# An fp32 encoder trunk on one core: the q and k heads are turned by VectorE's block transposes instead of TensorE, and the first two output tiles are interleaved

## Chip, cores and metric

One NeuronCore of one Trainium2 chip. The metric is the device time of one execution in microseconds, the median of several. Lower is better.

## What is computed

Two pre-norm transformer layers over 256 tokens of width 2048, all in float32. The first layer's attention has two kinds of heads: A (8 heads, neighbourhood attention with a bias) and B (8 query heads, 2 key/value heads, with axial rotation). The second layer has C (12 query heads, 4 key/value heads, a window and a sink logit) and D (3 groups of 4 query heads, 4 key/value heads, masked by stride), both with a rotation of the first 32 of 128 dimensions. After each attention comes a SwiGLU block of hidden width 5632.

```
for layer in range(DEPTH):
    xn = rms_norm(x, attn_norm[layer])
    x = x + mixer(xn, w_in, w_out, ...)     # q, k: rms_norm by head, gain, rotation
    x = x + swiglu(rms_norm(x, ffn_norm[layer]), w_gate[layer], w_up[layer], w_down[layer])
```

## The kernel before

**Units and ticks.** All weights (some 390 MB) stream through a ring of four slots. A unit is two chunks of 128 rows by 512 columns of a weight matrix. SP loads it to `w_raw`; ScalarE copies it to `w_hi` in the rounded format that TensorE multiplies fast; VectorE subtracts to get `w_lo` (`split`); TensorE's `unit` then runs 12 matmuls, for 2 token blocks x 2 chunks x 3 products (hi*hi, hi*lo, lo*hi). Eight units make a tile of 512 columns in the input and output projections. ScalarE can split unit u only when TensorE is done with unit u-4, and VectorE follows it, so both run at most some three units ahead of TensorE. One unit is one tick of the attention plan.

**The input projection.** Layer one has 9 tiles (`AB_TILES`: kv_b, q_b, q_b, q_a, k_a, v_a, q_a, k_a, v_a), layer two 10 (`CD_TILES`: k_d, q_d, q_d, q_d, k_c, v_c, q_c, q_c, q_c, v_d). All accumulate in PSUM pair 0. While TensorE multiplies the next tile, a finished q or k tile goes through these steps, `qk_tick(p, n)` being unit n of the tile behind it:
- ScalarE's `evacuate` copies the accumulators to `stage[0]`, scaled by the row's norm. It stands in ScalarE's queue before the split of unit 3, and can start once TensorE is done with the first token block of the tile's last unit. The first matmul of the next tile waits for it (`acc_free`).
- unit 0: ScalarE squares `stage[0]` to `stage[1]`.
- unit 1: VectorE sums the squares by head (L971); GpSimd makes `head_rstd` from them (L1153, L1156).
- unit 2: VectorE scales by `head_rstd` into `stage[2]` (L976) and, but for A's heads, rotates into `stage[0]` (`rotate_axial`, `rotate_partial`).
- unit 3 or 4 (`turn_tick`): TensorE transposes the 4 heads x 2 token blocks by eight matmuls with the identity (L431) into the two banks `t_bank`; one unit later ScalarE copies them to `qt_*` or `kt_*` (L694, L696; A's gains ride on this copy).

VectorE's and ScalarE's `attention(t)` stands in their queues three units behind the split, that is behind `split` of unit t+3.

**Items.** One item is one query head (one slot of three groups for D). `AB_ITEMS` and `CD_ITEMS` give its ticks: scores on TensorE; a tick later VectorE's row maxima; a tick later ScalarE's exponentials; then VectorE's division (`probs`); the transposes of `probs` on TensorE; two ticks later (or one) the product with v; ScalarE's and VectorE's hi/lo split of its result to `ht_hi`, `ht_lo` (L676, L964). Score banks are PSUM 2 to 4, taken in turn.

**The output projection.** Four tiles of 8 units. The first runs beside the last items, and each of its units waits (`ot_ready`) for the heads it reads. Each finished tile goes through `residual_add` (VectorE), four groups of four block transposes one unit apart (`turn`, L882), `residual_hi` and `residual_ssq` (ScalarE), `residual_lo` (VectorE). The same is done behind the down projection. At a change of stage the next stage's units wait for the last tile's `xt_lo` (`tile_split`).

Of the kernel before, what the change touches and what calls it, by code (L numbers as in the profile page):

```python
# [32 lines left out]
P = 128  # L33
# [4 lines left out]
DH = 128  # L38
# [25 lines left out]
AB_ITEMS = ([("b", h, 22 + 2 * h, 27 + 2 * h, 29 + 2 * h) for h in range(8)]  # L64
            + [("a", h, t, t + 4, t + 6) for h, t in enumerate((45, 47, 49, 51, 68, 69, 70, 71))])
CD_ITEMS = ([("d", s, 37 + 4 * s, 42 + 4 * s, 80 + s) for s in range(4)]
            + [("c", h, *ticks) for h, ticks in enumerate(
                [(61, 65, 67), (63, 67, 69), (65, 69, 71), (67, 71, 73), (69, 73, 75), (71, 76, 77), (73, 77, 78),
                 (74, 78, 79), (76, 80, 82), (77, 81, 83), (78, 82, 84), (79, 83, 85)])])
# [6 lines left out]

class Mixer:


    def __init__(self, tiles, items, chunks, fills, heads_before, qk_before, last_users):  # L80
        self.tiles, self.items, self.chunks = tiles, items, chunks
        self.ticks = KU * (len(tiles) + 1)
# [6 lines left out]
        for t in range(self.ticks + 8):  # L89
            for p in self.qk_tiles:  # L90
                if t == self.turn_tick(p):
                    for half in range(2):
                        self.fill["qk", p, half] = fills
                        fills += 1
# [6 lines left out]
        assert not {at for *_, at, _ in items} & {self.turn_tick(p) for p in self.qk_tiles}
# [7 lines left out]
        for n, (kind, h, *_) in enumerate(items):  # L109
            self.banks.append([0, 1, 2] if kind == "d" else [n % 3])  # L110
# [28 lines left out]
def plan():  # L139


    ph, u, a, b, f, th = {}, 0, 0, 0, 2 * XT, 2 * XT
# [3 lines left out]
    for layer, (tiles, items, chunks) in enumerate(((AB_TILES, AB_ITEMS, AB_CHUNKS), (CD_TILES, CD_ITEMS, CD_CHUNKS))):  # L146
        m = Mixer(tiles, items, chunks, f, heads, qk, last_users)
# [5 lines left out]
        u, a, th = u + KU * XT, a + XT, th + 2 * XT  # L153
# [21 lines left out]
def encoder(nc, x, attn_gain, ffn_gain, ab_w_in, ab_w_out, a_gain, a_bias, b_gain, cd_w_in, cd_w_out,  # L175
# [3 lines left out]
    with ExitStack() as ctx:  # L179
# [27 lines left out]
        gain_a = sb("gain_a", [P, 2])  # L207
        sink_sb = sb("sink_sb", [P, 12])
# [1049 lines left out]
```

## Time and profile before

| | |
|---|---|
| median of 3 runs | 2148.21 us (2148.09 to 2148.26) |
| the profiled execution | 2148.37 us, span 2146.6 us |
| TensorE busy | 2129.5 us, 99% |
| VectorE busy | 1380.5 us, 64% |
| ScalarE busy | 1001.7 us, 47% |
| GpSimd busy | 65.8 us, 3% |
| DMA | 399 MB, mean 186 GB/s |

Busy is the union of an engine's instructions. Matmuls overlap in the records (each some 0.39 us long, started 0.23 us apart), so what one costs is read from the distance of starts. "Idle before" is the engine's idle time just before an instruction, with what ended it.

### The profile page before, as it was taken

Reading aid. Unit: us, or ns where it says so; the run is one execution under the profiler, and the core shown is the slowest. Engines: PE = TensorE matmul, PEld = TensorE weight load, DVE = VectorE, ACT = ScalarE, POOL = GpSimd, SP = SyncE. Lnnn points to the kernel's source line nnn. Section 1 sums busy time; section 2 is a strip of 40 time slices with the busy share of each in tenths; the row PEclk is TensorE's granted clock in tenths of the full one; section 3 lists DMA queues with packets and bytes.
Section 4 is the critical chain, followed back from the end, with each engine's and each line's share of the span. In section 5 each row is a group of like instructions: output and inputs, shape, how many; then the busy total and the mean of one; then the engine's idle time right before and its main releaser. Section 6 shows DMA issues by size and latency. Waiting matters only on the chain.

```text
span 2146.6 us, 28247 instructions
## 1 busy us (share of the span) xinstructions
PE 2129.5 (99%) x9540; PEld 1760.2 (82%) x9540; DVE 1380.5 (64%) x1807; ACT 1001.7 (47%) x1270; POOL 65.8 (3%) x55
## 2 busy tenths in 40 slices
PE   8999999999999999999999999999999999999999
PEld 7888888888888888888888778888888888888887
DVE  5755587676666766666666666786676666765443
ACT  6555555444444444444455556454444444444443
POOL 0000010000000000000011010000000000000000
PEclk9999999999999999999999999999999999999999
DMA  8545556666666665555665453466666666656654
GB/s 275 167 147 172 172 176 196 195 183 191 204 195 182 190 204 185 186 190 193 210 192 176 147 158 118 157 199 194 194 183 191 203 195 183 189 189 203 215 201 141
DMA packets 207805, 399.32 MB, mean 186 GB/s; under 512 B 13312, under 2 KB 13568, under 8 KB 207744
## 3 DMA queue, kind: packets, MB, share of 16 engines
q1 hardware_dynamic: 205296, 394.30, 59.4%
q10 hardware_dynamic: 2448, 4.21, 0.6%
q8 instruction: 37, 0.61, 0.1%
q14 instruction: 24, 0.20, 0.0%
HBM read 396.37 MB, written 2.10 MB: 186 GB/s over the span
## 4 chain that ended last, share of the span: by engine, by line
PE 96%; DVE 2%; ACT 1%; issue 0%; POOL 0%; DMA 0%; SPq 0%; ACTq 0%; DVEq 0%
PE psum L411 31%; PE psum L414 31%; PE psum L412 31%; PE psum L501 2%; PE psum L431 1%; PE psum L479 1%; ACT w_hi L578 1%; DVE w_lo L836 1%; DVE turn_sb L882 0%; POOL head_rstd L1156 0%; PE psum L499 0%; DMA x_res<-in_x 0%; ACT xt_hi L621 0%; DVE xt_lo L894 0%; DVE stage L976 0%
## 5 line engine op out<-in xcount | busy, mean ns | idle before, releaser
L836 DVE TENSOR_TENSOR w_lo<-w_raw,w_hi 128x1024 fp32r<-128x1024 f32 x760 | 908.5, 1202 | 625.8 <-ACT w_hi L578 620.4
L578 ACT ACTIVATE w_hi<-w_raw 128x1024 fp32r<-128x1024 f32 x760 | 786.3, 1041 | 937.0 <-PE psum L414 925.1
L411 PE MATMUL psum<-w_hi,xt_hi 128*128 128x512 f32 x2016 | 795.6, 395 | 3.8 <-DVE xt_lo L894 3.6
L414 PE MATMUL psum<-w_hi,xt_lo 128*128 128x512 f32 x2016 | 785.5, 390 | 0.0
L412 PE MATMUL psum<-w_lo,xt_hi 128*128 128x512 f32 x2016 | 784.8, 389 | 0.0
L411 PEld LDWEIGHTS psum<-w_hi,xt_hi 128*128 128x128 f32 x2016 | 378.8, 188 | 83.4 <-DVE xt_lo L894 4.8
L414 PEld LDWEIGHTS psum<-w_hi,xt_lo 128*128 128x128 f32 x2016 | 378.6, 188 | 79.7
L412 PEld LDWEIGHTS psum<-w_lo,xt_hi 128*128 128x128 f32 x2016 | 378.9, 188 | 77.8
L411 PE MATMUL psum<-w_hi,ht_hi 128*128 128x512 f32 x960 | 376.1, 392 | 0.0
L414 PE MATMUL psum<-w_hi,ht_lo 128*128 128x512 f32 x960 | 373.7, 389 | 0.0
L412 PE MATMUL psum<-w_lo,ht_hi 128*128 128x512 f32 x960 | 373.6, 389 | 0.0
L882 DVE STREAM_TRANSPOSE turn_sb<-stage 32x256 f32<-32x256 f32 x544 | 236.9, 436 | 8.8
L411 PEld LDWEIGHTS psum<-w_hi,ht_hi 128*128 128x128 f32 x960 | 180.2, 188 | 37.6
L414 PEld LDWEIGHTS psum<-w_hi,ht_lo 128*128 128x128 f32 x960 | 180.2, 188 | 37.6
L412 PEld LDWEIGHTS psum<-w_lo,ht_hi 128*128 128x128 f32 x960 | 180.2, 188 | 37.4
L909 DVE SCALAR_TENSOR_TENSOR stage<-psum,rstd,stage 128x512 f32<-128x512 f32 x44 | 33.1, 751 | 52.0 <-PE psum L414 52.0
L644 ACT ACTIVATE ht_hi<-turn_sb 128x512 f32 (+1 forms) x44 | 25.4, 625 | 79.1 <-DVE turn_sb L882 79.1
L1163 POOL COPY x_res<-stage 128x1024 f32 x12 | 22.4, 1863 | 922.1 <-DVE stage L867 922.1
L867 DVE TENSOR_TENSOR stage<-psum,x_res 128x512 f32<-128x512 f32 x32 | 22.1, 691 | 30.9 <-PE psum L414 30.9
L621 ACT ACTIVATE xt_hi<-turn_sb,gain_x 128x256 f32 (+1 forms) x48 | 20.5, 499 | 43.4 <-DVE turn_sb L882 43.4
L637 ACT ACTIVATE stage<-psum,rstd 128x512 f32<-128x512 f32 x44 | 30.1, 689 | 18.2 <-PE psum L414 18.2
L1156 POOL TENSOR_TENSOR head_rstd<-head_eps,minus_half 128x8 f32<-128x8 f32 (+1 forms) x15 | 36.3, 2418 | 1.2
(98 smaller groups left out, 606.7 us busy)
## 6 DMA issues: line engine op xcount, KB each, us to landing
w_raw<-in_w_gate SPq DMA_DIRECT2D x176, 512.0 KB, 3.7
w_raw<-in_w_up SPq DMA_DIRECT2D x176, 512.0 KB, 3.8
w_raw<-in_w_down SPq DMA_DIRECT2D x160, 512.0 KB, 4.2
w_raw<-in_cd_w_in SPq DMA_DIRECT2D x80, 512.0 KB, 3.8
w_raw<-in_ab_w_in SPq DMA_DIRECT2D x72, 512.0 KB, 3.7
w_raw<-in_ab_w_out SPq DMA_DIRECT2D x32, 512.0 KB, 3.6
w_raw<-in_cd_w_out SPq DMA_DIRECT2D x32, 512.0 KB, 3.6
w_raw<-in_w_down SPq DMA_DIRECT2D x32, 256.0 KB, 2.6
```

What stands on the lines that cost most here:

```text
L411: nc.tensor.matmul(acc, hi[:, chunk, ts], w_hi[:, slot, c, :], start=first and c == 0, stop=False)
L412: nc.tensor.matmul(acc, hi[:, chunk, ts], w_lo[:, slot, c, :], start=False, stop=False)
L414: mm = nc.tensor.matmul(acc, lo[:, chunk, ts], w_hi[:, slot, c, :], start=False, stop=end)
L501: mm = nc.tensor.matmul(dst, qt[:, qh, tok * P:tok * P + P], kt[:, kh, :], start=kind in "ab", stop=True)
L578: nc.scalar.activation(w_hi[:, slot, 0:n, :], w_raw[:, slot, 0:n, :], ACT.Copy).then_inc(hi_ready, 1)
L637: ins = nc.scalar.activation(stage[0][:, tok, :], ACC[0][:, tok, :], ACT.Silu, scale=rstd[:, 2 * layer + 1, tok:tok + 1])
L644: nc.scalar.activation(ht_hi[:, bass.ds(i * 4 + 2 * half, 2), :], turn_sb[:, 2 * half:2 * half + 2, :], ACT.Copy).then_inc(t_hi, 1)
L836: nc.vector.tensor_tensor(w_lo[:, slot, 0:n, :], w_raw[:, slot, 0:n, :], w_hi[:, slot, 0:n, :].bitcast(F32), ALU.subtract).then_inc(lo_rea ...
L882: ins = nc.vector.transpose(dst[32 * r:32 * r + 32, q], src[32 * q:32 * q + 32, r])
L909: ins = nc.vector.scalar_tensor_tensor(out=stage[1][:, tok, :], in0=ACC[1][:, tok, :], scalar=rstd[:, 2 * layer + 1, tok:tok + 1], in1=sta ...
L1156: nc.gpsimd.tensor_tensor(head_rstd[:, :, 0:nh], head_eps[:, :, 0:nh], half, ALU.pow).then_inc(hrstd_ready, 1)
L1163: nc.gpsimd.tensor_copy(x_res[:, :, bass.ds(n * N, N)], stage[0][:]).then_inc(x_stored, 1)
```

## The change

- `turn_heads`: for each q or k tile VectorE does 16 block transposes of 32 partitions x 8 x 32, four in each of the units 3 to 6 of the next tile, from `stage` straight to `qt_*` and `kt_*`, whose layout is now by token block. TensorE's transposes of q and k heads and ScalarE's copies of them go, and with them the second transpose bank.
- `evacuate` of a q or k tile waits for `qk_turned` of the q or k tile before it.
- A's two gains become one product, which ScalarE multiplies onto `kt_a` in place (`k_scaled`), at unit 7.
- The sum of squares, GpSimd's power and the scaling by `head_rstd` are done by token block, in two halves.
- The four output tiles are written out unit by unit (`OUT_UNITS`): tiles 0 and 1 take turns, four units each, tile 1 in PSUM pair 1; then tiles 2 and 3. Tile 0's four groups of `turn` are done in two units.
- Items start 3 or 4 ticks later; the last 4 (layer one) or 8 (layer two) use two score banks in turn; the second o bank goes; one transpose bank is left for `probs`.
- The last tile's `residual_lo` stands one unit earlier, ahead of `mean_square`.

```diff
-AB_ITEMS = ([("b", h, 22 + 2 * h, 27 + 2 * h, 29 + 2 * h) for h in range(8)]
-            + [("a", h, t, t + 4, t + 6) for h, t in enumerate((45, 47, 49, 51, 68, 69, 70, 71))])
+AB_ITEMS = ([("b", h, 25 + 2 * h, 30 + 2 * h, 32 + 2 * h) for h in range(8)]
+            + [("a", h, t, t + 4, t + 6) for h, t in enumerate((48, 50, 52, 54, 72, 73, 74, 75))])
...
+OUT_UNITS = [(n, k) for half in range(2) for n in range(2) for k in range(4 * half, 4 * half + 4)]
+OUT_UNITS += [(n, k) for n in range(2, XT) for k in range(KU)]
+OUT_END = [max(i for i, (tile, _) in enumerate(OUT_UNITS) if tile == n) for n in range(XT)]
+PAIR_UNITS = 2 * KU
...
-            self.banks.append([0, 1, 2] if kind == "d" else [n % 3])
+            late = n - len(items) + (4 if layer == 0 else 8)
+            self.banks.append([0, 1, 2] if kind == "d" else [n % 3] if late < 0 else [2 + late % 2 * 2])
...
             def attention(layer, t):    # TensorE
                 m = mixers[layer]
-                for q, p in enumerate(m.qk_tiles):
-                    if t == m.turn_tick(p):
-                        _, kind, h0 = m.tiles[p]
-                        pe.wait_ge(qk_normed, m.qk0 + q + 1)
...
-                                transposes(lambda c, tok: src[:, tok, (2 * half + c) * P:(2 * half + c + 1) * P], f)
...
+                    if kind[0] in "qk":    # ScalarE, evacuate
+                        act.wait_ge(qk_turned, m.qk0 + m.qk_rank[p])
...
-                                ins = nc.scalar.activation(qk_dest(kind, h0, half), src, ACT.Copy)
...
+                    if kind == "k_a" and t == m.qk_tick(p, 7):
+                        act.wait_ge(qk_turned, m.qk0 + q + 1)
+                        tile = kt_a[:, h0 // 4].rearrange("p t c i -> p (t c i)")
...
+                        nc.scalar.activation(tile, tile, ACT.Copy, scale=gain_qk[:]).then_inc(k_scaled, 1)
...
+            def turn_heads(layer, q, kind, h0, a):
+                if a == 0:
+                    dve.wait_ge(qk_normed, mixers[layer].qk0 + q + 1)
+                nh = 2 if kind == "kv_b" else 4
+                heads = heads_of(stage[2 if kind in ("q_a", "k_a") else 0], nh)
+                for b in range(4):
+                    src = heads[32 * a:32 * a + 32, :, :, 32 * b:32 * b + 32]
+                    dst = qk_tile(kind, h0)[32 * b:32 * b + 32, :, :, 32 * a:32 * a + 32]
+                    ins = nc.vector.transpose(dst, src)
+                if a == 3:
+                    ins.then_inc(qk_turned, 1)
...
+                    a = t - m.qk_tick(p, 3)
+                    if 0 <= a < 4:
+                        turn_heads(layer, q, kind, h0, a)
...
+                for i in range(len(OUT_UNITS)):    # VectorE
+                    for n in range(XT - 1):
+                        if i == OUT_END[n] + LEAD:
+                            residual_add(layer, "out", n)
+                    split(po["u"] + i, i % RING)
+                    if i < PAIR_UNITS:
+                        attention(layer, KU * len(m.tiles) + i - LEAD)
+                    for n in range(XT - 1):
+                        late = i - OUT_END[n] - LEAD
+                        if n == 0 and 0 <= late < 2:
+                            turn(layer, "out", n, 2 * late)
+                            turn(layer, "out", n, 2 * late + 1)
+                        elif n and 0 <= late < 4:
+                            turn(layer, "out", n, late)
+                        if late == (3 if n == 0 else 5):
+                            residual_lo(layer, "out", n)
...
+                    for tok in range(TOK):    # GpSimd
+                        pool.wait_ge(hssq_ready, TOK * (m.qk0 + q) + tok + 1)
+                        step.then(nc.gpsimd.tensor_scalar(head_eps[:, tok, 0:nh], head_ssq[:, tok, 0:nh], 1.0 / DH, EPS,
+                                                          ALU.mult, ALU.add))
+                        nc.gpsimd.tensor_tensor(head_rstd[:, tok, 0:nh], head_eps[:, tok, 0:nh], minus_half[:, 0:nh],
+                                                ALU.pow).then_inc(hrstd_ready, 1)
```

ScalarE's order at the end of the second layer's second tile (`q_d`, heads 0 to 3); L578 is the split, L666 the evacuation, L683 the squares. Before:

```order
L578 ACTIVATE w_hi<-w_raw 128x1024 [waits unit_used,w_loaded0]
L696 ACTIVATE kt_d<-psum 128x512 [waits t_full] x2
L578 ACTIVATE w_hi<-w_raw 128x1024 [waits unit_used,w_loaded1]
L578 ACTIVATE w_hi<-w_raw 128x1024 [waits unit_used,w_loaded2]
L666 ACTIVATE stage<-psum,rstd 128x512 [waits acc0_done]
L666 ACTIVATE stage<-psum,rstd 128x512 [waits unit_used]
L578 ACTIVATE w_hi<-w_raw 128x1024 [waits unit_used,w_loaded3]
L683 ACTIVATE stage<-stage 128x1024 [waits acc0_free]
```

The same place in the changed kernel (L566, L656 and L673 are the same lines there):

```order
L566 ACTIVATE w_hi<-w_raw 128x1024 [waits unit_used,w_loaded0]
L566 ACTIVATE w_hi<-w_raw 128x1024 [waits unit_used,w_loaded1]
L566 ACTIVATE w_hi<-w_raw 128x1024 [waits unit_used,w_loaded2]
L656 ACTIVATE stage<-psum,rstd 128x512 [waits acc0_done,qk_turned]
L656 ACTIVATE stage<-psum,rstd 128x512 [waits unit_used]
L566 ACTIVATE w_hi<-w_raw 128x1024 [waits unit_used,w_loaded3]
L673 ACTIVATE stage<-stage 128x1024 [waits acc0_free]
```

The copies of the transposed heads are gone, and the evacuation has a second wait.

VectorE's order for a q_d tile, from the scaling on; L836 is the split. Before:

```order
L836 TENSOR_TENSOR w_lo<-w_raw,w_hi 128x1024 [waits hi_ready]
L976 TENSOR_TENSOR stage<-stage,head_rstd 128x1024 [waits hrstd_ready]
L944 TENSOR_TENSOR stage<-stage,partial_sb 128x8x32 [waits dve_step]
L947 TENSOR_TENSOR stage<-stage,partial_sb 128x8x16 x2
L951 TENSOR_TENSOR stage<-stage,cd_gain_sb 128x8x96
L952 TENSOR_TENSOR stage<-stage 128x8x32 [waits dve_step]
L836 TENSOR_TENSOR w_lo<-w_raw,w_hi 128x1024 [waits hi_ready] x7
```

In the changed kernel, where L816 is the split:

```order
L975 TENSOR_TENSOR stage<-stage,head_rstd 128x512 [waits hrstd_ready] x2
L924 TENSOR_TENSOR stage<-stage,partial_sb 128x8x32 [waits dve_step]
L927 TENSOR_TENSOR stage<-stage,partial_sb 128x8x16 x2
L931 TENSOR_TENSOR stage<-stage,cd_gain_sb 128x8x96
L932 TENSOR_TENSOR stage<-stage 128x8x32 [waits dve_step]
L816 TENSOR_TENSOR w_lo<-w_raw,w_hi 128x1024 [waits hi_ready]
L944 STREAM_TRANSPOSE qt_d<-stage 32x8x32 [waits qk_normed]
L944 STREAM_TRANSPOSE qt_d<-stage 32x8x32 x3
L816 TENSOR_TENSOR w_lo<-w_raw,w_hi 128x1024 [waits hi_ready]
L944 STREAM_TRANSPOSE qt_d<-stage 32x8x32 x4
```

Two more such pairs of a split and four transposes follow, then three splits.

VectorE's order in the output stage. Before, every tile's residual has the same form; the last tile's, in the first units of the up projection, layer one:

```order
L867 TENSOR_TENSOR stage<-psum,x_res 128x512 [waits unit_used]
L836 TENSOR_TENSOR w_lo<-w_raw,w_hi 128x1024 [waits hi_ready]
L882 STREAM_TRANSPOSE turn_sb<-stage 32x8x32 [waits acc0_free,t_hi]
L882 STREAM_TRANSPOSE turn_sb<-stage 32x8x32 x3
L836 TENSOR_TENSOR w_lo<-w_raw,w_hi 128x1024 [waits hi_ready]
L882 STREAM_TRANSPOSE turn_sb<-stage 32x8x32 x4
```

The changed kernel from the add of tile 0 to that of tile 1 (L847 is the add, L862 the turn, L874 `residual_lo`):

```order
L847 TENSOR_TENSOR stage<-psum,x_res 128x512 [waits unit_used]
L816 TENSOR_TENSOR w_lo<-w_raw,w_hi 128x1024 [waits hi_ready]
L862 STREAM_TRANSPOSE turn_sb<-stage 32x8x32 [waits acc0_free,t_hi]
L862 STREAM_TRANSPOSE turn_sb<-stage 32x8x32 x7
L816 TENSOR_TENSOR w_lo<-w_raw,w_hi 128x1024 [waits hi_ready]
L862 STREAM_TRANSPOSE turn_sb<-stage 32x8x32 x8
L816 TENSOR_TENSOR w_lo<-w_raw,w_hi 128x1024 [waits hi_ready] x2
L874 SCALAR_TENSOR_TENSOR xt_lo<-turn_sb,gain_x,xt_hi 128x256 [waits t_hi,turned]
L874 SCALAR_TENSOR_TENSOR xt_lo<-turn_sb,gain_x,xt_hi 128x256
L874 SCALAR_TENSOR_TENSOR xt_lo<-turn_sb,gain_x,xt_hi 128x256 [waits t_hi]
L874 SCALAR_TENSOR_TENSOR xt_lo<-turn_sb,gain_x,xt_hi 128x256
L847 TENSOR_TENSOR stage<-psum,x_res 128x512 [waits acc1_done,ssq_done,x_stored]
```

Sixteen transposes lie between three splits, and tile 1's add stands right behind tile 0's `xt_lo`.

## Rows read from the trace of the kernel before

**Rows 1.** The page's first part: busy us (share of the span) x instructions.

```profile
PE 2129.5 (99%) x9540; PEld 1760.2 (82%) x9540; DVE 1380.5 (64%) x1807; ACT 1001.7 (47%) x1270; POOL 65.8 (3%) x55
```

**Rows 2.** Waits view, TensorE: who for whom, us in total, times, longest.

```profile
PE psum L411 <- DVE xt_lo L894: 3.6, 3, 1.2
PE psum L431 <- DVE probs L1027: 1.3, 1, 1.3
PE psum L431 <- DVE stage L938: 0.9, 1, 0.9
...
PE psum L499 <- ACT probs L714: 0.5, 1, 0.5
```

**Rows 3.** Timeline, TensorE: start us, us, instruction; a tile's first two units.

```profile
1105.89 0.39 PE L411 MATMUL psum<-w_hi,xt_hi 128*128 128x512 f32 x1
...
1108.61 0.39 PE L411 MATMUL psum<-w_hi,xt_hi 128*128 128x512 f32 x1
```

**Rows 4.** Timeline, TensorE, around a group of q head transposes.

```profile
1119.27 0.39 PE L414 MATMUL psum<-w_hi,xt_lo 128*128 128x512 f32 x1
1119.50 1.03 PE L431 MATMUL psum<-ident_sb,stage 128*128 128x128 f32 x8
1120.29 0.48 PE L411 MATMUL psum<-w_hi,xt_hi 128*128 128x512 f32 x1
1120.60 0.40 PE L412 MATMUL psum<-w_lo,xt_hi 128*128 128x512 f32 x1
```

**Rows 5.** Groups by line and form, TensorE: busy us, mean ns.

```profile
L431 PE MATMUL psum<-ident_sb,stage 128*128 128x128 f32 x112 | 14.6, 273 | 0.9 <-DVE stage L938 0.9
```

**Rows 6.** Timeline, VectorE, residual's turn at a change of stage.

```profile
342.31 1.77 DVE L882 STREAM_TRANSPOSE turn_sb<-stage 32x256 f32<-32x256 f32 x4
344.10 1.23 DVE L836 TENSOR_TENSOR w_lo<-w_raw,w_hi 128x1024 fp32r<-128x1024 f32 x1
345.35 1.78 DVE L882 STREAM_TRANSPOSE turn_sb<-stage 32x256 f32<-32x256 f32 x4
```

**Rows 7.** Timeline, VectorE, squares, scaling and rotation of a q_d tile.

```profile
1111.11 1.21 DVE L971 TENSOR_REDUCE head_ssq<-stage 128x8 f32<-128x1024 f32 x1
1112.69 1.23 DVE L836 TENSOR_TENSOR w_lo<-w_raw,w_hi 128x1024 fp32r<-128x1024 f32 x1 [0.37 <-ACT w_hi L578]
1115.44 1.23 DVE L976 TENSOR_TENSOR stage<-stage,head_rstd 128x1024 f32<-128x1024 f32 x1 [1.53 <-POOL head_rstd L1156]
...
1118.78 2.35 DVE L836 TENSOR_TENSOR w_lo<-w_raw,w_hi 128x1024 fp32r<-128x1024 f32 x2
```

**Rows 8.** Groups by line and form, GpSimd.

```profile
L1156 POOL TENSOR_TENSOR head_rstd<-head_eps,minus_half 128x8 f32<-128x8 f32 x14 | 35.3, 2518 | 1.2
...
L1156 POOL TENSOR_TENSOR head_rstd<-head_eps,minus_half 128x4 f32<-128x4 f32 x1 | 1.0, 1014 | 0.1
```

**Rows 9.** Timeline, ScalarE, evacuation of a tile.

```profile
1106.09 0.69 ACT L666 ACTIVATE stage<-psum,rstd 128x512 f32<-128x512 f32 x1 [0.67 <-PE psum L414]
```

**Rows 10.** Timeline, VectorE, scaling and axial rotation of q_b.

```profile
67.79 1.23 DVE L976 TENSOR_TENSOR stage<-stage,head_rstd 128x1024 f32<-128x1024 f32 x1 [1.53 <-POOL head_rstd L1156]
...
72.79 2.35 DVE L836 TENSOR_TENSOR w_lo<-w_raw,w_hi 128x1024 fp32r<-128x1024 f32 x2
```

**Rows 11.** Timeline, VectorE, an item of C.

```profile
1271.90 0.15 DVE L1020 TENSOR_TENSOR denom<-denom,sinkexp 128x2 f32<-128x2 f32 x1
...
1272.82 0.68 DVE L1010 TENSOR_REDUCE rowmax<-psum 128x2 f32<-128x512 f32 x1
1273.54 0.23 DVE L1012 TENSOR_SCALAR negmax<-rowmax,neg_sink 128x2 f32<-128x2 f32 x1
```

**Rows 12.** Timeline, TensorE, transposes and product of an item.

```profile
1272.96 0.66 PE L431 MATMUL psum<-ident_sb,probs 128*128 128x128 f32 x4 [1.33 <-DVE probs L1027]
1273.45 1.03 PE L479 MATMUL psum<-cd_pt,v_c 128*128 128x256 f32 x4
1274.32 0.27 PE L499 MATMUL psum<-mask_sb,ident_sb 128*128 128x256 bf16 x1
```

**Rows 13.** Timeline, TensorE, matmuls of the opening.

```profile
12.38 0.63 PE L414 MATMUL psum<-w_hi,xt_lo 128*128 128x512 f32 x1
12.81 0.63 PE L411 MATMUL psum<-w_hi,xt_hi 128*128 128x512 f32 x1
```

More of the change, by code:

```diff
@@ L88, in __init__ @@
         self.fill = {}
[L89 to L94, printed above, removed]
+        for t in range(self.ticks):
             for n, (_, _, _, at, _) in enumerate(items):
@@ L99, in __init__ @@
         self.fills = fills
[L101 removed]
+        self.qk_rank = {p: q for q, p in enumerate(self.qk_tiles)}
         self.pv = sorted(range(len(items)), key=lambda n: (items[n][4], n))
@@ L146, in plan @@
     for layer, (tiles, items, chunks) in enumerate(((AB_TILES, AB_ITEMS, AB_CHUNKS), (CD_TILES, CD_ITEMS, CD_CHUNKS))):
-        m = Mixer(tiles, items, chunks, f, heads, qk, last_users)
+        m = Mixer(layer, tiles, items, chunks, f, heads, qk, last_users)
         mixers.append(m)
@@ L376, in _ @@
             for layer in range(2):
-                for p, (col, _, _) in enumerate(mixers[layer].tiles):
+                m = mixers[layer]
+                for p, (col, _, _) in enumerate(m.tiles):
                     for k in range(KU):
@@ L749, in _ @@
                 m, pi, po, pu, pd = mixers[layer], *(ph[s, layer] for s in ("in", "out", "up", "down"))
-                def out_tile(n, first):
-                    for k in range(KU):
-                        if k == LEAD and first:
-                            evacuate(layer, len(m.tiles) - 1)
-                        split(n * KU + (po["u"] + k), k % RING)
-                        if first:
-                            attention(layer, KU * len(m.tiles) + k - LEAD)
-                        elif k == LEAD + 2:
-                            residual_ssq(layer, "out", n - 1)
-                        elif k == LEAD + 3:
-                            residual_hi(layer, "out", n - 1)
                 for p in range(len(m.tiles)):
@@ L1037, in _ @@
                 m, pi, po, pu, pd = mixers[layer], *(ph[s, layer] for s in ("in", "out", "up", "down"))
-                def out_tile(n, first):
-                    for k in range(KU):
-                        if k == LEAD - 1 and not first:
-                            residual_add(layer, "out", n - 1)
-                        split(n * KU + (po["u"] + k), k % RING)
-                        if first:
-                            attention(layer, KU * len(m.tiles) + k - LEAD)
-                        elif LEAD - 1 <= k < LEAD + 3:
-                            turn(layer, "out", n - 1, k - LEAD + 1)
-                        elif k == LEAD + 4:
-                            residual_lo(layer, "out", n - 1)
                 for p in range(len(m.tiles)):
```

234 lines of the change are left out of this document (108 added, 126 removed).

## Prediction

> **What bounds the kernel now.** I read the page's first part, then who TensorE waits for, then the timelines of TensorE, VectorE, ScalarE and GpSimd around one tile. The page says that TensorE is busy 2129.5 of 2146.6 us [rows 1]. The waits view says that behind the opening it waits a handful of times only: 3.6 us in three waits on `xt_lo`, 1.3 on `probs`, 0.9 on a q tile that VectorE had not rotated in time, 0.5 on an exponential [rows 2]. So whatever leaves TensorE's queue shortens the program by its full length, and whatever makes TensorE wait lengthens it by its full length. VectorE is at 64% over the span [rows 1], but that mean says nothing here: the question is whether it is in time at the few points where TensorE waits for it. The unit of all sums is the tick: one weight unit of 12 matmuls, 1105.89 to 1108.61, so 2.72 us [rows 3].
>
> **What is taken off TensorE.** A tile's eight q/k head transposes sit between matmuls. Two matmuls of the stream start 0.23 us apart; around a group the starts are 1119.27, 1119.50 (the group), 1120.29, 1120.60 [rows 4]: 1.33 us from the last before to the second after, where 0.46 would do, so 0.87 a group. The 112 transposes [rows 5] are 14 groups, 12.2 us, and k/v of B with four transposes gives about 0.45 more: **12.7 us**. The waits of 0.9 (it is the wait of such a group), 1.3 and 0.5 go with their places: up to **2.7 us**. ScalarE loses 30 copies out of PSUM and gains two scalings; TensorE does not wait for these copies, so I cost that at nothing; what covers them is ScalarE's idle time.
>
> **The three late `xt_lo`.** The last tile's `residual_lo` now stands one unit earlier, ahead of `mean_square`, at the three changes of stage where TensorE waits 3.6 us in all [rows 2]. VectorE had a free unit there, so I take the **3.6 us** as gone (bounds 0 and 3.6).
>
> **What is put on VectorE.** 16 block transposes a tile, four in each of the units 3 to 6. The nearest rows are the same instruction with the same 32x256 shape in the residual's turn: a group of four takes 1.80 us from its start to the next split (342.31 to 344.10), the split itself 1.25 (344.10 to 345.35) [rows 6]. So a unit with a turn in it takes VectorE 3.05 us, and the tick is 2.72: **during the four units VectorE can't make up lateness, it loses another 0.33 a unit**. The Trainium skill, VectorE: DVE Perf Modes, "The three transpose paths" and "Rules for kernel authors", says that VectorE transposes 32x32 blocks only and advises TensorE for 128x128 where PSUM will do. Its rule speaks against the change in direction; the rows put the same exchange at 0.87 us of TensorE against 7.2 us of VectorE [rows 4, 6].
>
> **The new wait.** ScalarE's `evacuate` of a q or k tile now waits for `qk_turned` of the tile before, since the block transposes read `stage` directly where eight TensorE transposes had freed it at unit 4. The next tile's first matmul waits for that evacuation (one accumulator pair). The deadline is thus TensorE's end of the tile. Worked on the second tile of the second layer (q_d, heads 0 to 3), behind which TensorE starts the third at 1105.89 [rows 3]:
> - VectorE's sum of squares starts at 1111.11; the scaling by `head_rstd` starts at 1115.44, behind GpSimd's power; the rotation ends at 1118.78 [rows 7]. The halves by token help: the power takes 2.52 us for 8 values and 1.01 for 4 [rows 8]. With 0.68 for half the squares, 0.38 for the step before the power and 1.2 a power, the second token's value is there at 1114.8 (1111.11 + 0.68 + 0.38 + 1.2 + 0.2 + 1.2). Its scaling (0.65) and the rotation's 2.1 follow: the end is about 1.1 earlier than now, at 1117.65.
> - Four units with turns: 4 x 3.05 = 12.2, so `qk_turned` comes at 1129.85.
> - Evacuation of the first token 0.69 [rows 9] and two hand-overs of about 0.05 to 0.1: 1130.7.
> - TensorE, without its group of transposes, would be ready for the fourth tile at 1105.89 + 8 x 2.72 = 1127.65.
>
> **It waits 3.05 us to save 0.87.** Bounds: 4.2 where the halved power brings nothing, 2.3 where no power is waited for (squares, split, scaling, rotation back to back). Four tiles of the second layer are like this (k_d and the three q_d): **12.2 us**.
>
> The other tiles, by the same sum plus VectorE's items and minus TensorE's:
> - q_b heads 0 to 3: the axial rotation is longer (67.79 to 72.79, 5.00 against 3.34 for the partial one, so 1.66 more) [rows 7, 10]: **4.7**.
> - q_b heads 4 to 7: 4.7, plus 2.6 us of VectorE item work, less about 4 us of TensorE item work between the units: **3.4**.
> - q_a and the first k_a: rotation none, many items on TensorE: 0. kv_b is half a tile: 0.
> - second k_a: the tile behind it is v, without the wait, but ScalarE scales `kt_a` first (about 1.05) and then evacuates: 1.0 for the wait, 1.05 for the scaling: **2.0**.
> - c tiles (three q_c): VectorE's item work is 0.92 us for reciprocal and two scalings and about 0.9 for the maxima [rows 11], with a split and a turn 4.9 a unit; TensorE has 2.72 plus 0.87 for each product with v and 0.5 for a transpose [rows 12]. Where an item comes every tick this is 4.1. Both sides are close; d3's probabilities now fall beside a q tile's squares; score banks are reused after two items instead of three. I work out about 2.2 for d3's `probs`, 3.4 at the first q_c and 6 from there to the end of the heads: **11.5**, the weakest term (3 to 18).
> - Output tiles: tile 0's four turn groups are done in two units, tile 1 ends four units behind tile 0 and not eight. From tile 0's last matmul VectorE needs 0.75 + 1.2 + 3.6 + 1.2 + 3.6 + 1.2 = 11.6 us until unit 16 is split, which TensorE wants after 4 x 2.72 = 10.9; then `residual_lo`, the wait for ScalarE's sum of squares and tile 1's turns at 3.05 a unit with no reserve left. I get 3.5 a layer, **7.0** (3 to 12).
>
> **Sum.** Waits 12.2 + 4.7 + 3.4 + 2.0 + 11.5 + 7.0 = 40.8; savings 12.7 + 2.7 + 3.6 = 19.0. Net **+21.8 us** on the profiled execution's 2148.37, which is 0.16 over the median of 2148.21: **2170 us**. The small ends (9.2, 3.9, 2.6, 1.2, 3, 3: 23 us of waits) give 2152, the large ones (16.8, 5.9, 4.5, 2.9, 18, 12: 60 us) 2189. A measurement of this kernel tells about 0.2% (4.3 us) from no change.
>
> **Rivals.**
> 1. *The turns are in time* (faster). Mechanism: `qk_turned` comes before TensorE's end of the tile, so only the savings remain: 2148.2 - 19.0 = 2129; with the two output tiles' waits 2136. It decides at a group of four transposes of 1.05 us: 1117.65 + 4 x (1.25 + 1.05) + 0.8 = 1127.65. The shape's 1.8 [rows 6] speaks against it, and nothing in the profile for it but that source and destination differ a little from the residual's. Chance 0.09.
> 2. *The gaps also cost the clock.* TensorE would idle 3 to 5 us some eight times; the longest idle time of before outside the opening is far shorter. At the opening, behind idle time, matmuls start 0.43 us apart (12.38, 12.81) [rows 13], the lower level of 1.2 GHz, against 0.23. If each long gap brings some eight matmuls at that pace, 0.2 us more for each, 8 x 1.6 = 13 us: 2183. The Trainium skill, TensorE: Matmul & The Clock Gate, "Why this matters for your kernels", warns that idle gaps between bursts of matmuls bring the lower clock back. By that rule this rival holds wherever a gap is long enough; no row of this trace has such a gap between matmuls, so it is open. Chance 0.15.
> 3. *Savings and waits cancel.* The waits come out at the small end or below since the items' work on TensorE covers them in both layers: 2144 to 2152. Against it stands that the four d tiles have no item beside them at all. Chance 0.07.
> 4. That the change doesn't do what it says is ruled out by the order: no transpose of `stage` is left on TensorE.
>
> **Numbers.** The forecast, with its own range 2152 to 2188, has 0.69. Range 2148 to 2189. Faster by over 0.2% 0.09 (rival 1), within 0.2% 0.05, slower 0.86.
>
> **What would show it.** In the changed kernel: waits of TensorE on ScalarE's evacuation at the start of the q_d tiles and k_c, some 3 us each, and ScalarE waiting on VectorE's transposes just before; the transposes at 0.44 us, 240 of them; the power of 4 values near 1.2 us; no wait on `xt_lo`; PEclk at 1.0 throughout, or not (rival 2); waits on `w_lo` behind unit 16 of the output stage. I am wrong if the four d tiles start on time, or if the block transposes take about half of what the residual's take.

## The result, and the profile after

| | before | after |
|---|---|---|
| median | 2148.24 us (2148.09 to 2149.57, 4 runs) | 2187.89 us (2187.61 to 2189.43, 4 runs) |
| ratio | | 1.0185, 95% interval 1.0167 to 1.0202 |
| the profiled execution | 2148.37 us, span 2146.6 | 2187.92 us, span 2185.7 |

The change costs 39.6 us. The forecast was 2170; the time lies 18 us above it, at the upper end of the range. The page's first part, as [rows 1]:

```profile
PE 2133.8 (98%) x9424; PEld 1754.6 (80%) x9424; DVE 1484.4 (68%) x2077; ACT 988.4 (45%) x1243; POOL 81.5 (4%) x85
```

TensorE has 116 instructions fewer and is yet 4 us longer busy: something in it got slower. VectorE has 104 us more. Who TensorE waits for, as [rows 2] (us in total, times, longest):

```profile
PE psum L425 <- ACT stage L656: 27.4, 8, 5.8
...
PE psum L445 <- DVE probs L1027: 4.0, 3, 1.8
PE psum L425 <- DVE w_lo L816: 3.2, 5, 0.9
PE psum L425 <- DVE stage L847: 3.0, 2, 1.5
PE psum L425 <- ACT v_a L654: 2.2, 1, 2.2
```

The evacuation (L656), for which the waits view of before has no row, is now waited for eight times, 27.4 us. The wait on `xt_lo` L894 has no successor. Now the second layer's first tile, `k_d`, whose heads VectorE turns while TensorE multiplies the next tile (q_d, heads 0 to 3). VectorE's timeline (start us, us, instruction, idle before):

```profile
1102.52 1.27 DVE L968 TENSOR_REDUCE head_ssq<-stage 128x4 f32<-128x512 f32 x2
...
1106.82 0.69 DVE L975 TENSOR_TENSOR stage<-stage,head_rstd 128x512 f32<-128x512 f32 x1 [0.90 <-POOL head_rstd L1152]
...
1109.62 1.22 DVE L816 TENSOR_TENSOR w_lo<-w_raw,w_hi 128x1024 fp32r<-128x1024 f32 x1
1110.76 1.78 DVE L944 STREAM_TRANSPOSE kt_d<-stage 32x256 f32<-32x256 f32 x4
1112.55 1.23 DVE L816 TENSOR_TENSOR w_lo<-w_raw,w_hi 128x1024 fp32r<-128x1024 f32 x1
1113.81 1.78 DVE L944 STREAM_TRANSPOSE kt_d<-stage 32x256 f32<-32x256 f32 x4
...
1118.66 1.23 DVE L816 TENSOR_TENSOR w_lo<-w_raw,w_hi 128x1024 fp32r<-128x1024 f32 x1
1119.91 1.79 DVE L944 STREAM_TRANSPOSE kt_d<-stage 32x256 f32<-32x256 f32 x4
```

No idle time stands between 1106.82 and 1121.70 (a third split and group are left out): the groups come 3.05 us apart, as worked out from [rows 6]. ScalarE's timeline at the same place:

```profile
1121.74 1.26 ACT L656 ACTIVATE stage<-psum,rstd 128x512 f32<-128x512 f32 x2 [4.08 <-DVE kt_d L944]
```

And TensorE's timeline, from the last matmul of q_d, heads 0 to 3, on:

```profile
1118.84 0.39 PE L428 MATMUL psum<-w_hi,xt_lo 128*128 128x512 f32 x1
1122.57 0.77 PE L425 MATMUL psum<-w_hi,xt_hi 128*128 128x512 f32 x1 [3.35 <-ACT stage L656]
1123.14 0.63 PE L426 MATMUL psum<-w_lo,xt_hi 128*128 128x512 f32 x1
1123.56 0.63 PE L428 MATMUL psum<-w_hi,xt_lo 128*128 128x512 f32 x1
1123.99 0.63 PE L425 MATMUL psum<-w_hi,xt_hi 128*128 128x512 f32 x1
...
1125.64 0.40 PE L426 MATMUL psum<-w_lo,xt_hi 128*128 128x512 f32 x1
1125.87 0.39 PE L428 MATMUL psum<-w_hi,xt_lo 128*128 128x512 f32 x1
```

TensorE is done with that tile at 1119.2, ScalarE is held until the last transpose, and the next matmul starts 3.73 us after the last one. Then comes the second cost: the matmuls behind the gap start 0.43 us apart (1123.14, 1123.56, 1123.99), as in [rows 13], and only from 1125.64 on 0.23 apart. The windows view shows it as a granted clock (stretch, its length, busy us of PE, PEld, DVE, ACT and POOL, then PEclk, DMA share, GB/s):

```profile
1118.84:1122.57 3.73, 0.39 (x2) 0.03 (x1) 3.63 (x6) 0.83 (x2) 0.00 (x0) 0.94 0.64 204
1122.57:1125.50 2.93, 2.93 (x7) 2.35 (x8) 1.62 (x2) 2.33 (x3) 0.00 (x0) 0.50 0.58 157
1125.50:1145.59 20.09, 20.09 (x89) 16.62 (x89) 15.96 (x27) 7.42 (x7) 3.25 (x4) 1.00 0.52 150
```

0.50 is 1.2 GHz, 1.00 is 2.4. Behind the opening there are seven such stretches, each behind an idle gap: of 5.01 us (q_b, heads 0 to 3), 5.79 (q_b, heads 4 to 7), 2.19 (`v_a`) and 3.34 or 3.35 (the four D tiles). 48 matmuls of the stream start some 0.43 us apart in them. A gap of 3.05 us at the first q_c and one of 1.85 before it are followed by none.

### The profile page after: what moved, and what is told of

It is laid out like the page before. It is cut to its first block, busy times and chain, and to the rows that moved or that the text cites. A ratio compares the mean times of both kernels' runs of the same rounds, so it can differ in the third digit from the quotient of the medians.

```text
span 2185.7 us, 27698 instructions
## 1 busy us (share of the span) xinstructions
PE 2133.8 (98%) x9424; PEld 1754.6 (80%) x9424; DVE 1484.4 (68%) x2077; ACT 988.4 (45%) x1243; POOL 81.5 (4%) x85
## 4 chain that ended last, share of the span: by engine, by line
PE 85%; DVE 11%; ACT 2%; POOL 1%; issue 1%; DMA 0%; SPq 0%; ACTq 0%; DVEq 0%
PE psum L425 27%; PE psum L428 27%; PE psum L426 27%; DVE w_lo L816 3%; DVE turn_sb L862 1%; PE psum L471 1%; PE psum L494 1%; POOL head_rstd L1152 1%; DVE qt_d L944 1%; DVE qt_c L944 1%; ACT w_hi L566 1%; PE psum L445 1%; DVE qt_b L944 1%; POOL head_eps L1150 0%; DVE stage L975 0%
## 5 line engine op out<-in xcount | busy, mean ns | idle before, releaser
L816 DVE TENSOR_TENSOR w_lo<-w_raw,w_hi 128x1024 fp32r<-128x1024 f32 x760 | 909.6, 1202 | 573.8 <-ACT w_hi L566 567.6
L566 ACT ACTIVATE w_hi<-w_raw 128x1024 fp32r<-128x1024 f32 x760 | 786.3, 1040 | 953.4 <-PE psum L428 928.5
L425 PE MATMUL psum<-w_hi,xt_hi 128*128 128x512 f32 x2016 | 797.6, 396 | 27.8 <-ACT stage L656 27.4
L862 DVE STREAM_TRANSPOSE turn_sb<-stage 32x256 f32<-32x256 f32 x544 | 236.9, 436 | 8.7
L847 DVE TENSOR_TENSOR stage<-psum,x_res 128x512 f32<-128x512 f32 x32 | 21.7, 690 | 33.6 <-PE psum L428 33.6
L609 ACT ACTIVATE xt_hi<-turn_sb,gain_x 128x256 fp32r<-128x256 f32 (+1 forms) x48 | 20.5, 498 | 52.4 <-DVE turn_sb L862 52.4
L1152 POOL TENSOR_TENSOR head_rstd<-head_eps,minus_half 128x4 f32<-128x4 f32 (+1 forms) x30 | 33.7, 1123 | 2.5
L1164 POOL COPY x_res<-stage 128x1024 f32 x4 | 7.4, 1859 | 693.5 <-DVE stage L847 693.5
```

Of the source, the lines that this page charges most:

```text
L425: nc.tensor.matmul(acc, hi[:, chunk, ts], w_hi[:, slot, c, :], start=first and c == 0, stop=False)
L566: nc.scalar.activation(w_hi[:, slot, 0:n, :], w_raw[:, slot, 0:n, :], ACT.Copy).then_inc(hi_ready, 1)
L816: nc.vector.tensor_tensor(w_lo[:, slot, 0:n, :], w_raw[:, slot, 0:n, :], w_hi[:, slot, 0:n, :].bitcast(F32), ALU.subtract).then_inc(lo_rea ...
L862: ins = nc.vector.transpose(dst[32 * r:32 * r + 32, q], src[32 * q:32 * q + 32, r])
L1152: nc.gpsimd.tensor_tensor(head_rstd[:, tok, 0:nh], head_eps[:, tok, 0:nh], minus_half[:, 0:nh], ALU.pow).then_inc(hrstd_ready, 1)
```

## The experiments

Each time is a median beside runs of the kernel before on the same chip (2148.73 in the first set, 2148.76 in the others). The changed kernel's 2187.89 stood beside 2148.24, so a difference to it, as given below, is uncertain by that 0.5 us.

**1. Keep TensorE at work in the gaps.** Ahead of the waiting first matmul stand matmuls whose result nobody reads, into a PSUM bank that is free.

```diff
+                        if k == 0:
+                            fill_in(FILL.get((layer, p), 0))
                         unit(pi["u"] + t, k % RING, xt_hi, ...)
```

> The changed kernel with 8 to 22 extra matmuls (each 0.23 us, into a bank that nothing reads) in TensorE's queue ahead of the eight first matmuls that wait for an evacuation, and one of v_a: work in place of idle time, deadlines unchanged. Theory (idle gaps cost twice, once as waiting and once because the clock falls behind them): the granted clock is 1.00 throughout, the idle time left at these places is about 1 us or less each, the time falls by the price of 27.3 us at half the clock, some 13 us, to about 2175. Rival (the low clock of the changed kernel lies in idle time and costs nothing): no gain, 2188 or a little more for fillers that come late.

Measured: 2187.93 us (2186.92 to 2188.25), no gain. The forecast failed because two of the eight groups stood at tiles that wait for nothing, where they cost 4.4 and 2.6 us of work, and two real gaps (5.81 and 3.04 us) stayed open, each with a stretch at the lower level of 6.8 us behind it. The time is the one that the rival named, but not for its reason, so it settled nothing; it was repeated with the groups at the right tiles.

```diff
-            FILL = {(0, 2): 20, (0, 3): 22, (0, 9): 8, (1, 2): 13, (1, 3): 13, (1, 4): 13, (1, 5): 13, (1, 7): 12}
+            FILL = {(0, 3): 22, (0, 4): 24, (0, 9): 8, (1, 2): 14, (1, 3): 14, (1, 4): 14, (1, 5): 14, (1, 8): 13}
```

> The changed kernel with fillers (matmuls whose result nobody reads) ahead of the first matmul of the tiles that wait, this time at the right ones: 22 at q_b 0's evacuation, 24 at q_b 4's, 8 at v_a's, 14 at each of the four D tiles, 13 at the first q_c, and none where nothing waits. In the first version two of eight groups stood at tiles that do not wait. They cost 4.4 and 2.6 us, and two of the uncovered gaps kept 13.6 us of the lower clock level, against 27.3 us in all in the changed kernel, so gain and cost cancelled. My theory (13.6 us of the changed kernel's time is the clock behind the long gaps, the rest is waits): no interval of the lower level before the end, waits as before but filled, 2174 (2172 to 2178). Rival (fillers only shift where the clock drops, or the waits are longer than they look): 2183 or more with the lower level still present.

Measured: 2178.02 us (2176.95 to 2180.24), 9.9 less than the changed kernel and at the upper edge of the forecast (2172 to 2178), ratio to before 1.0136 (1.0120 to 1.0151). The windows view at `k_d`'s end, first of the changed kernel, then with fillers:

```profile
1118.00:1130.00 12.00, 8.65 (x33) 6.77 (x32) 7.93 (x12) 4.46 (x6) 0.00 (x0) 0.86 0.59 174
```

```profile
1118.00:1130.00 12.00, 11.83 (x53) 9.48 (x52) 8.16 (x11) 6.34 (x7) 3.25 (x4) 1.00 0.68 186
```

All seven stretches at the lower level are gone. Set side by side unit by unit, the two traces differ in the first unit behind each gap: 1.45, 1.79, 1.59, 1.37, 1.59, 1.58 and 1.60 us, **11.0 us** in all. The distance from the last matmul of the stream before a gap to the first behind it is the same in both (3.73 and 3.73 us at `k_d`), so the fillers change nothing but the pace behind it. One new stretch came, against the forecast, behind a gap of 1.85 us ahead of late probabilities, and costs 1.6. The 11.0 us are the clock's share. My 13.6 was half of the 27.3 us in which the lower level was granted; but some 3.7 of them fall into idle time, where a low clock costs nothing.

**2. A second `stage` buffer.** Evacuation waits for the turns of two tiles back.

```diff
-        stage = [sb(f"stage{k}", [P, TOK, N]) for k in range(3)]
+        stage = [sb(f"stage{k}", [P, TOK, N]) for k in range(4)]
...
-                if kind[0] in "qk":
-                    act.wait_ge(qk_turned, m.qk0 + m.qk_rank[p])
+                g = m.qk0 + m.qk_rank.get(p, 0)
+                if kind[0] in "qk" and g > 1:
+                    act.wait_ge(qk_turned, g - 1)
```

> The changed kernel with a second stage buffer: q and k tiles are evacuated to the two in turn, so an evacuation waits for the turn of the tile before the last. Theory (the wait for qk_turned is what costs): TensorE's 27.4 us on the evacuation go, the clock stays at 1.00, and what is left are the output tiles' 6 us and some us at the items: 2142 to 2152. Rival (VectorE is simply full, its work of a q_d tile being about 21.6 us of 21.8): the waits come back as waits for w_lo or probs, 2160 to 2175.

Measured: 2163.81 us (2163.40 to 2164.03), 24.1 less, 1.0070 (1.0055 to 1.0086): the theory's 2142 to 2152 was missed, the time is in the rival's range. Its waits:

```profile
PE psum L448 <- DVE probs L1033: 8.1, 5, 2.1
...
PE psum L428 <- ACT stage L660: 4.5, 2, 4.4
```

The evacuation's waits fall from 27.4 to 4.5 us, those on probabilities rise from 4.0 to 8.1, and four stretches at the lower level are left (22 matmuls of the stream). So the evacuation's wait for the turns was the main cost: without it 24.1 of the 39.6 us are gone, part of them the clock behind the gaps that closed. The kernel is still slower than before: some waits came back as waits for probabilities, as the rival said, by 4.1 us. The wait of 4.4 us that is left at q_b (heads 4 to 7) has another cause, which ScalarE's timeline of this run shows:

```profile
113.08 0.47 ACT L713 ACTIVATE probs<-psum,negmax 128x256 f32<-128x256 f32 x1 [4.25 <-DVE negmax L1021]
...
113.99 1.26 ACT L660 ACTIVATE stage<-psum,rstd 128x512 f32<-128x512 f32 x2
```

In ScalarE's queue an item's exponential stands ahead of the evacuation, and it waits for maxima that VectorE takes only after its turns. No buffer helps there.

**3. How much is one group of transposes worth?** `k_d` keeps four groups, the three q_d tiles have three, two and one; ScalarE writes the rest of `qt_d` untransposed, so D's scores are not the reference's.

```diff
+        GROUPS = {("k_d", 0): 4, ("q_d", 0): 3, ("q_d", 4): 2, ("q_d", 8): 1}
...
+                if a >= groups:
+                    return
```

> The changed kernel with all four groups of block transposes for k_d, three for the first q_d tile, two for the second, one for the third; the parts of those tiles that are not turned are filled by a plain copy on ScalarE, so D's scores are not those of the reference. Theory (deadline: the last group of transposes against TensorE's end of the tile): TensorE waits 3.35, 1.55 (one group of 1.8 less), 0 and 0 us for the evacuations behind them; each missing group also takes away nothing but its own 1.8 us. Rival (the wait comes from ScalarE's own queue or from GpSimd's power): 3.3 in all four.

Measured, one run: 2173.03 us. The gaps are 3.34, 0.28, 0 and 0 us, where the theory had said 3.35, 1.55, 0 and 0 and the rival 3.3 in all four. TensorE at the tile with three groups:

```profile
1145.99 0.39 PE L430 MATMUL psum<-w_hi,xt_lo 128*128 128x512 f32 x1
1146.66 0.47 PE L427 MATMUL psum<-w_hi,xt_hi 128*128 128x512 f32 x1 [0.28 <-ACT stage L658]
1146.97 0.40 PE L428 MATMUL psum<-w_lo,xt_hi 128*128 128x512 f32 x1
1147.21 0.39 PE L430 MATMUL psum<-w_hi,xt_lo 128*128 128x512 f32 x1
```

A group is worth 3.06 us, not its own 1.78: the split in front of the last group leaves the path with it. And the matmuls behind a gap of 0.28 keep their pace.

**4. Two groups of turns behind one split.** If that is so, the same 16 transposes in two units instead of four must end 2.5 us earlier.

```diff
-                    if 0 <= a < 4:
-                        turn_heads(layer, q, kind, h0, a)
+                    if 0 <= a < 2:
+                        turn_heads(layer, q, kind, h0, 2 * a)
+                        turn_heads(layer, q, kind, h0, 2 * a + 1)
```

> The changed kernel with the four groups of turns done in two units, two groups behind one split, as the output stage's tile 0 has it. In the changed kernel a group of 1.78 us stands behind each of four splits of 1.23 us with no idle time of VectorE between them; two splits would come after the last group instead of before it. My theory (the wait is VectorE's own work in order, and a group removed took its split with it): the last group ends 2.5 us earlier, the four D tiles wait 0.85 us each in place of 3.35, q_b 0, q_b 4 and the first q_c 2.5 less each, so 17.5 us less waits; most gaps are then under 2 us and 7 to 12 us of clock come back: 2158 to 2164. Rival (VectorE has no slack, two groups in one unit make the split late and TensorE waits for w_lo instead): 2176 to 2188, with waits on w_lo of some 1 to 2 us a tile.

Measured: 2174.23 us (2172.78 to 2175.43), 13.7 less, 1.0120 (1.0104 to 1.0135). Neither the theory (2158 to 2164) nor the rival (2176 to 2188) had the number. The waits:

```profile
PE psum L445 <- DVE probs L1028: 13.0, 5, 5.1
PE psum L425 <- ACT stage L656: 9.3, 6, 1.8
```

The evacuation's share fell by 18.1 us (I had said 17.5), and the wait on `w_lo`, which the rival named, rose by 1.6 only. What neither had seen are the items: VectorE at the first q_c,

```profile
1284.72 3.57 DVE L944 STREAM_TRANSPOSE qt_c<-stage 32x256 f32<-32x256 f32 x8
1288.30 1.22 DVE L816 TENSOR_TENSOR w_lo<-w_raw,w_hi 128x1024 fp32r<-128x1024 f32 x1
1289.56 3.59 DVE L944 STREAM_TRANSPOSE qt_c<-stage 32x256 f32<-32x256 f32 x8
...
1293.57 0.61 DVE L1028 TENSOR_SCALAR probs<-probs,rdenom 128x256 f32<-128x256 f32 x2
```

so the probabilities that TensorE wants at 1289.2 come at 1294.2, a gap of 5.09 us. What a group gains for the evacuation it takes from the division behind it. At the four D tiles, where no item is near, the pairing helps: their gaps are 1.28, 1.82, 1.57 and 1.40 us, at the price of one wait of 0.62 us on `w_lo`, and no stretch at the lower level follows them.

**5. Token halves undone** in the changed kernel: one sum of squares, one power, one scaling.

```diff
-                    for tok in range(TOK):
-                        pool.wait_ge(hssq_ready, TOK * (m.qk0 + q) + tok + 1)
+                    pool.wait_ge(hssq_ready, m.qk0 + q + 1)
```

> The changed kernel with the token halves undone: one sum of squares, one pair of GpSimd instructions, one scaling a tile, as in the kernel before. If the halves bring the chain of a tile forward by the difference of the pow chains (2518+1014 ns in one piece against two overlapped halves), the last group of turns ends some 0.5 to 1.2 us later, at each of 8 waiting tiles, so 2192 to 2198. Rival (VectorE is full between the sum of squares and the last turn, and fills the wait for the power with a split): no difference, 2186 to 2190.

Measured: 2190.87 us (2189.45 to 2192.82), 3.0 more than the changed kernel, or 2.1 by the two ratios; their intervals (1.0179 to 1.0211 here, 1.0167 to 1.0202 there) overlap, so the traces must decide. Three of the four D gaps are 3.91 us instead of 3.35 (the other is 2.50). From the sum of squares to the end of the rotation it is 7.7 us (1105.18 to 1112.85) against 7.1 (1102.52 to 1109.62). So the halves bring 0.6 us a tile, at the low end of what I expected, and the run's time lies between my 2192 to 2198 and the rival's 2186 to 2190. In the profiled execution all idle time of TensorE grew by only 1.6 us (49.7 against 48.1), while three of its seven stretches at the lower level last 6.8 us, where the changed kernel has one such: some 12 more matmuls 0.43 us apart, 2.5 us. So more of the loss in that execution is clock than waiting. GpSimd in the changed kernel shows why the halves bring no more:

```profile
1103.57 1.01 POOL L1152 TENSOR_TENSOR head_rstd<-head_eps,minus_half 128x4 f32<-128x4 f32 x1
1104.66 0.72 POOL L1150 TENSOR_SCALAR head_eps<-head_ssq 128x4 f32<-128x4 f32 x1
1105.46 1.33 POOL L1152 TENSOR_TENSOR head_rstd<-head_eps,minus_half 128x4 f32<-128x4 f32 x1
```

The second half's step before the power takes 0.72 us, and its power 1.33.

**6. The useful part alone.** The kernel before, with `residual_lo` one unit earlier at the three changes of stage (one of them shown):

```diff
-                        if layer == 1 and p == 0 and k == LEAD + 4:
+                        if layer == 1 and p == 0 and k == LEAD + 3:
                             residual_lo(0, "down", XT - 1)
-                        if layer == 1 and p == 0 and k == LEAD + 3:
                             mean_square(2)
```

> The kernel before with one part of the change alone: the last residual_lo one unit earlier at the three changes of stage. Theory: the three waits on xt_lo (3.6 us idle, 4.0 between starts) go: 2144.2. Rival (ScalarE's xt_hi is the later one, so the wait only changes its name): 2148.

Measured: 2144.22 us (2143.38 to 2145.38, 11 runs), 0.9980 (0.9971 to 0.9989); the 3.6 us of waits on `xt_lo` L894 are gone from the waits view and nothing took their place. With the token halves added:

> The kernel before with two parts of the change alone: residual_lo one unit earlier at the changes of stage, and the token halves of sum of squares, power and scaling. The first alone gave 2144.22. The halves can take the waits that the kernel before has on a head's normalization and on the late probabilities (0.9 and 1.3 us), if they come from GpSimd's power: 2142 to 2143. Rival (they come from VectorE's order, and 14 more GpSimd pairs and VectorE instructions cost what they bring): 2144 to 2145.

Measured: **2143.10 us** (2142.29 to 2143.96, 9 runs), 0.9974 (0.9964 to 0.9984). The two intervals overlap, so the times alone do not show that the halves bring 1.1 us more; that rests on the waits view, where 0.9 on the rotated head became 0.4 and 1.3 on the probabilities 0.8:

```profile
PE psum L431 <- DVE probs L1031: 0.8, 1, 0.8
PE psum L499 <- ACT probs L714: 0.5, 1, 0.5
PE psum L431 <- DVE stage L938: 0.4, 1, 0.4
```

This version is faster than both kernels.

**7. Both faults mended at once**: two buffers, and fillers at the gaps that those leave.

```diff
+            FILL = {(0, 4): 18, (0, 9): 8}
+            FILL_ITEM = {(0, 30): 8, (1, 46): 8, (1, 58): 7}
```

> The second stage buffer and the fillers together: fillers only at the gaps that the two-buffer kernel still has (18 at q_b 4's evacuation, 8 at v_a's, 8, 8 and 7 ahead of three late sets of probabilities). If the parts add up (my theory: the evacuation waits and the clock are two separate terms), the four intervals of the lower level go and with them 1.4 to 1.8 us each: 2157 to 2160 against 2163.8 of the two buffers alone, still 9 to 12 us slower than before, because the waits for late items and the output stage stay. Rival (fillers cost what they bring, or the lower level turns up behind the next shorter gap, as it did once in the last run): 2162 to 2165.

Measured: 2159.00 us (2158.66 to 2160.06), 1.0047 (1.0031 to 1.0064), as forecast. No stretch at the lower level is left behind the opening, and 4.8 us went against the two buffers alone. The gains of the two mends can't simply be added (9.9 and 24.1 make 34.0, together they brought 28.9), because the second buffer alone had already closed gaps with a stretch behind them: four stretches are left of seven. What remains, some 10 us over before, was not taken apart by a run; the trace has gaps at the items and output tiles, and the fillers themselves.

## Why the prediction was right or wrong

The direction and the mechanism held, and the time lies in the range. But the forecast's number was 18 us short: 11.0 of them are rival 2, which came true beside the forecast, some 5 are restarts and small waits that the sum did not have, and 1.2 are savings counted too high. The forecast's own range, 2152 to 2188, took in rival 2's 2183 as well, so the number alone could not have told the two apart; the granted clock and experiment 1 do. Term by term, on the profiled executions:

| term | forecast | measured |
|---|---|---|
| four D tiles | 12.2 | 13.4 |
| q_b, heads 0 to 3 | 4.7 | 5.0 |
| q_b, heads 4 to 7 | 3.4 | 5.8 |
| second k_a and `v_a` | 2.0 | 2.2 |
| C | 11.5 | 8.3 |
| output tiles, both layers | 7.0 | 5.9 |
| sum of waits | 40.8 | 40.6 |
| TensorE's transposes | -12.7 | -11.5 |
| waits of before | -2.7 | -2.8 |
| `xt_lo` | -3.6 | -3.6 |
| clock behind the gaps | 0 | 11.0 |
| net | 21.8 | 33.7 |

That the sum of waits came out within 0.2 us is luck: C was 3.2 and the output tiles (by idle time) 1.1 too high, q_b (heads 4 to 7) 2.4 and the D tiles 1.2 too low.

The spans differ by 39.1. Of the 5.4 us that the table lacks, some 2.3 are the restarts: a gap shows as 3.35 us of idle time, but the starts lie 3.73 apart where 0.23 would do, 0.15 more, the start after that can come up to 0.11 late, and the changed kernel has 18 such waits against 6. Another 2.9 are ten unit starts that come 0.1 to 0.4 us late, too short for a row in the waits view. Eight of them (2.2 us) stand beside the output stage's turns of tile 1:

```profile
320.95 1.23 DVE L816 TENSOR_TENSOR w_lo<-w_raw,w_hi 128x1024 fp32r<-128x1024 f32 x1
...
321.80 0.39 PE L428 MATMUL psum<-w_hi,ht_lo 128*128 128x512 f32 x1
...
322.23 0.19 PEld L425 LDWEIGHTS psum<-w_hi,ht_hi 128*128 128x128 f32 x1 [0.46 <-DVE w_lo L816]
322.23 0.50 PE L425 MATMUL psum<-w_hi,ht_hi 128*128 128x512 f32 x1
```

VectorE's split ends at 322.18, and the unit starts at 322.23, 0.43 us behind the last matmul and not 0.23, with 0.11 more at the next start: the 0.33 us a unit that the prediction had for a VectorE without reserve, paid by TensorE. With them the output tiles cost 8.1 us and not 5.9. The other two are short waits for an evacuation: of q_b, heads 0 to 3, held by kv_b's turns, and of the first `v_a`.

- **D tiles: right.** The sum gave 3.05, the trace 3.35 (3.50 by the starts). The rotation took 7.1 us from the sum of squares on where I had 6.54 (GpSimd's second half is slower than the row of the first, experiment 5), and the rest as worked out: groups 3.05 us apart, evacuation, hand-over. Rival 1 needed a group of 1.05 us; the block transposes to `qt_*` take 0.436 us each, as the residual's [rows 6].
- **q_b, heads 4 to 7: the sum ended too early.** It had 2.6 us of VectorE item work and took 4 us of TensorE's off. Up to the last turn the items cost VectorE 2.3 us (0.8 ahead of the first split with a turn behind it, 1.5 between 107.14 and 108.67), and TensorE some 4.2. But the last turn ends at 114.76, and the evacuation starts only at 117.36, 2.6 us later, which the sum did not have. ScalarE's queue has an item's exponentials before it, and these wait for maxima that stand in VectorE's queue behind the last turn and a division:

```profile
112.97 1.79 DVE L944 STREAM_TRANSPOSE qt_b<-stage 32x256 f32<-32x256 f32 x4
114.79 0.17 DVE L1024 RECIPROCAL rdenom<-denom 128x2 f32<-128x2 f32 x1
115.00 0.62 DVE L1027 TENSOR_SCALAR probs<-probs,rdenom 128x256 f32<-128x256 f32 x2
115.53 0.68 DVE L1010 TENSOR_REDUCE rowmax<-psum 128x2 f32<-128x512 f32 x1
116.24 0.17 DVE L1015 TENSOR_SCALAR negmax<-rowmax 128x2 f32<-128x2 f32 x1
```

ScalarE at the same place:

```profile
116.45 0.47 ACT L707 ACTIVATE probs<-psum,negmax 128x256 f32<-128x256 f32 x1 [4.26 <-DVE negmax L1015]
...
117.36 1.26 ACT L656 ACTIVATE stage<-psum,rstd 128x512 f32<-128x512 f32 x2
```

- **C: oversized.** Of my three parts, d3's `probs` came out at 1.85 us (2.2), the first q_c at 3.05 (3.4), and the items after it at 1.48 + 0.69 + 1.26 = 3.4 in place of 6. Why the last part was so much smaller no run shows.
- **Output tiles: right in place.** Three waits a layer: 0.64 and 0.87 us on `w_lo` behind tile 0's paired turns and behind tile 1's add, 1.48 on an accumulator that VectorE's add frees late. In the second layer 0.64, 0.80 and 1.50. With the late unit starts above it is 8.1 us for the 7.0 of the sum.
- **TensorE's transposes: 1.2 us too much.** By the measure of the prediction (from the last matmul of the stream before a place to the second behind it, less what two starts take, idle time taken off), all that stands between matmuls of the stream cost 95.4 us in 73 places before and 83.9 in 63 places after. The 15 groups account for 13.0 of that (0.90 us for one alone, 0.88 in company, 0.46 for the half one), so the price that I read from [rows 4] held; the items' own work costs some 1.5 us more in its new places.
- **Clock: the step that failed is leaving rival 2 out of the sum.** I had priced it well: eight matmuls, 1.6 us a gap, 13 us and 2183. It measured 1.37 to 1.79 a gap, 11.0 in all, and belonged with the forecast, not beside it, because the gaps that the forecast itself worked out were the condition. The row that I had, matmuls 0.43 us apart behind the opening's idle time [rows 13], was evidence for it, though of pace alone: the windows view prints a granted clock of 1.00 for the opening (12.00 to 13.00, before and after), where the trace has no record of the clock before 12.8. In the seven stretches pace and granted clock go together, 0.43 us with 0.50. The Trainium skill, TensorE: Matmul & The Clock Gate, "Why this matters for your kernels", warns against idle gaps between bursts of matmuls; these traces agree in that seven gaps of 2.19 to 5.79 us have the lower level behind them, though a gap of 3.05 us has not. A chance of 0.15 was too low.
- **`xt_lo`: right,** and the part of the change that pays by itself, with the token halves perhaps 1 us beside it (experiment 6).

## What to carry to other kernels

Moving work to an engine with 36% idle time is free only if the work ends before the next hand-over: count what stands in its queue between the data's arrival and that hand-over, splits included, and what stands ahead of the hand-over in the queue of the engine that makes it. If the sum says that TensorE will idle for microseconds, price the slower matmuls behind each gap too, from a place in the same trace where TensorE starts after a pause. And when a change of many parts loses, try its parts alone: one here was worth 0.20%, two together 0.26%.

## What the runs showed of the hardware

- Which gaps bring the lower level is not told by their length alone. In the changed kernel gaps of 2.19 and 3.35 us did, and one of 3.05 us did not; one of 1.85 us ahead of d3's probabilities did not in the changed kernel, and the same one did with two buffers, with paired turns, with groups left out and with the fillers at the right tiles. The gap at the first q_c, 3.05 us in the changed kernel, was 3.04 in the first run with fillers and had 6.8 us of the lower level behind it, some 14 matmuls. So each edit that shifts the program moves some 1.6 us or more in or out, which a comparison at this scale must allow for.
- The lower level costs less than half of the time in which it is granted when it begins in idle time: behind the gap of 5.79 us it was granted for 6.8 us, 3.0 of them before TensorE started again, and cost 1.8.
- Idle time in the profile understates what a wait costs TensorE: its matmul records overlap, so the starts lie 0.15 us further apart than idle time and pace together, and the unit start that came 0.2 us late (321.80 to 322.23) shows only 0.04 us of it.
- On GpSimd the same two instructions on the same 4 values took 0.19 and 1.01 us for the first token block and 0.72 and 1.33 for the second, which starts right behind; the mean of 28 powers is 1.12 us.
